# The last head group's probabilities go through DRAM like the others'; its scores are computed one weight granule earlier

## The reference, cut to what matters

```python
def moba_layer(x, norm_g, w_in, q_norm, k_norm, w_out):
    h = rms_norm(x, norm_g)
    q, k, v, z = jnp.split(h @ w_in, 4, axis=-1)      # w_in: 1024 x 8192
    q = rope(rms_norm(heads(q), q_norm))
    k = rope(rms_norm(heads(k), k_norm))
    v = heads(v)
    o = moba_attention(q, k, v)                        # softmax(q k^T * scale, causal) v
    return x + (o * jax.nn.silu(z)) @ w_out            # w_out: 2048 x 1024
```

## Time and profile before

| | |
|---|---|
| median of 3 runs | 412.7 us (412.46 to 412.87) |
| the profiled execution's own time | 412.65 us |
| its span | 410.7 us |
| TensorE busy in the span | 406.4 us (99%) |
| VectorE, ScalarE busy | 305.2 us (74%), 238.0 us (58%) |
| mean granted TensorE clock | 1.000 |

### The profile page before, as it was taken

How to read it: one execution, slowest core, us unless ns; L and a number is a source line. 1 busy time by engine, 2 the same in 40 slices (tenths; PEclk the granted TensorE clock), 3 DMA queues, 4 the chain that set the end, 5 groups by cost and what they waited for, 6 DMA issues and landing times.

```text
span 410.7 us, 5546 instructions
## 1 busy us (share of the span) xinstructions
PE 406.4 (99%) x2058; PEld 347.3 (85%) x2058; DVE 305.2 (74%) x405; ACT 238.0 (58%) x430; POOL 32.8 (8%) x45
## 2 busy tenths in 40 slices
PE   8999999999999999999999999999999999999996
PEld 8989889898888888888888888888888888888885
DVE  3879996978998855666836989569896699955622
ACT  5745553433735635677737696477965779646310
POOL 0167000000000000121000210010100200000000
PEclk9999999999999999999999999999999999999999
DMA  7996869756479975368896598995999879890002
GB/s 254 387 354 211 268 219 332 274 206 204 134 240 333 315 227 184 104 204 222 283 316 194 166 302 254 327 293 154 285 278 310 266 230 295 269 321 3 2 0 102
DMA packets 57466, 95.70 MB, mean 233 GB/s; under 512 B 9952, under 2 KB 19296, under 8 KB 57440
## 3 DMA queue, kind: packets, MB, share of 16 engines
q1 hardware_dynamic: 56720, 94.29, 71.9%
q10 hardware_dynamic: 720, 1.07, 0.8%
HBM read 84.07 MB, written 11.27 MB: 232 GB/s over the span
## 4 chain that ended last, share of the span: by engine, by line
PE 99%; DVE 0%; issue 0%
PE acc L739 26%; PE acc L741 26%; PE acc L740 26%; PE acc L762 3%; PE acc L784 3%; PE acc L783 3%; PE acc L781 3%; PE aux L874 2%; PE acc L803 1%; PE aux L739 1%; PE aux L741 1%; PE aux L740 1%; PE aux L892 1%; PE aux L893 1%; PE aux L891 1%; PE aux L873 1%
## 5 line engine op out<-in xcount | busy, mean ns | idle before, releaser
L951 DVE TENSOR_TENSOR w_lo<-raw,w_hi 128x2048 fp32r<-128x2048 f32 x65 | 147.9, 2280 | 25.7 <-ACT w_hi L472 25.7
L472 ACT ACTIVATE w_hi<-raw 128x2048 fp32r<-128x2048 f32 x64 | 121.9, 1912 | 46.1 <-PE acc L741 25.1
L739 PE MATMUL acc<-w_hi,hT_hi 128*128 128x512 f32 x320 | 127.9, 400 | 0.0
L741 PE MATMUL acc<-w_hi,hT_lo 128*128 128x512 f32 x320 | 124.8, 390 | 0.0
L740 PE MATMUL acc<-w_lo,hT_hi 128*128 128x512 f32 x320 | 124.6, 389 | 0.0
L741 PEld LDWEIGHTS acc<-w_hi,hT_lo 128*128 128x128 f32 x320 | 60.1, 188 | 13.0
L740 PEld LDWEIGHTS acc<-w_lo,hT_hi 128*128 128x128 f32 x320 | 60.2, 188 | 12.0
L739 PEld LDWEIGHTS acc<-w_hi,hT_hi 128*128 128x128 f32 x320 | 60.2, 188 | 11.8
L739 PE MATMUL acc<-w_hi,aT_hi 128*128 128x512 f32 x144 | 57.0, 396 | 0.0
L741 PE MATMUL acc<-w_hi,aT_lo 128*128 128x512 f32 x144 | 56.1, 390 | 0.0
L740 PE MATMUL acc<-w_lo,aT_hi 128*128 128x512 f32 x144 | 56.1, 389 | 0.0
(11 more groups left out here) (138 smaller groups left out, 477.0 us busy)
## 6 DMA issues: line engine op xcount, KB each, us to landing
raw<-in_w_in_dram SPq DMA_DIRECT2D x46, 1024.0 KB, 6.7
raw<-in_w_out_dram SPq DMA_DIRECT2D x16, 1024.0 KB, 5.3
raw<-in_w_pool_dram SPq DMA_DIRECT2D x4, 1024.0 KB, 7.8
wide<-between SPq DMA_DIRECT2D x32, 128.0 KB, 5.5
between<-wide SPq DMA_DIRECT2D x8, 512.0 KB, 3.4
p_between<-p_blocks SPq DMA_DIRECT2D x12, 192.0 KB, 4.3
p_blocks<-p_between SPq DMA_DIRECT2D x48, 48.0 KB, 2.6
raw<-in_w_in_dram SPq DMA_DIRECT2D x8, 256.0 KB, 7.9
```

Of the source, the lines that this page charges most:

```text
L472: act.activation(w_hi[:, slot, :], raw[:, slot, :], ACT.Copy).then_inc(hi_made, 1)
L739: pe.matmul(a, shi, whi, start=first and k == 0, stop=False)
L741: ins = pe.matmul(a, slo, whi, start=False, stop=last and k == GK - 1)
L951: dve.tensor_tensor(w_lo[:, slot, :], raw[:, slot, :], w_hi[:, slot, :].bitcast(F32), ALU.subtract).then_inc(w_split, 1)
```

## The change: what it does

The last group's probabilities take the path of the others: DVE turns them in 32x32 blocks, SP stores and fetches them, ACT copies them from `p_blocks`. The twelve PE transposes go. `scores(last, 0)` stands before out 0 instead of inside it; inside granule out j stands `attend(last, j + 1)`, with the values three steps behind the scores, so that values stay where they were and scores come one granule earlier. ACT and DVE have their last stage reordered. On SP, the fetch of the last group's k comes ahead of a weight load (it was behind), head 0's store and fetch stand around the fetch of y1, ahead of the load of out 7, and the other heads' come after all loads.

```diff
@@ SP, moves(g, j)
+                if (g, j) == (GROUPS, 0):
+                    store_p(g - 1, 0)
                 if j == 0 and g >= 2:
                     fetch_y1(g - 2)
+                if (g, j) == (GROUPS, 0):
+                    fetch_p(g - 1, 0)
...
-                if j == 6 and g < GROUPS:
+                if j == (6 if g < GROUPS - 1 else 5) and g < GROUPS:
                     fetch_k(g)
@@ SP, after the loads
+            last = GROUPS - 1
+            for h in range(1, HPG):
+                store_p(last, h)
+                fetch_p(last, h)
@@ ACT, exp_scores and probs_out
-                if g == GROUPS - 1 and h > 0:
-                    act.wait_ge(p_turned, h)
-                elif HPG * g + h > 0:
+                if HPG * g + h > 0:
                     act.wait_ge(p_blocked, HPG * g + h)
...
-                if g == GROUPS - 1:
-                    act.wait_ge(p_turned, h + 1)
-                else:
-                    act.wait_ge(p_landed, MOVED * (HPG * g + h + 1))
+                act.wait_ge(p_landed, MOVED * (HPG * g + h + 1))
                 if HPG * g + h > 0:
                     act.wait_ge(o_ready, HPG * g + h)
-                if g == GROUPS - 1:
-                    act.activation(probsT[:, :], aux[2][:, 0:3 * P], ACT.Copy).then_inc(pT_made, 1)
@@ ACT, last stage
-            for n in range(N_OUT1 + 3, N_END):
-                static_hi(n)
-                j = n - N_OUT1 - 3
-                if j < HPG:
-                    exp_scores(last, j)
-                if 1 <= j <= HPG:
-                    probs_out(last, j - 1)
+            exp_scores(last, 0)
+            for j in range(5):
+                static_hi(N_OUT1 + 3 + j)
+                if j + 1 < HPG:
+                    exp_scores(last, j + 1)
                 if j == 2:
                     y1_hi(last - 1)
+                if j >= 2:
+                    probs_out(last, j - 2)
+            probs_out(last, 3)
             y1_hi_last()
@@ PE
-            def turn_probs(g, h):
-                pe.wait_ge(exp_made, HPG * g + h + 1)
-                if h > 0:
-                    pe.wait_ge(pT_made, HPG * g + h)
-                for i in range(3):
-                    ins = pe.transpose(aux[2][:, i * P:(i + 1) * P], probs[:, i * P:(i + 1) * P], ident[:, :])
-                ins.then_inc(p_turned, 1)
...
             def attend(g, j):
-                late = 2 if g == GROUPS - 1 else 3
-                if j < HPG:
+                if 0 <= j < HPG:
                     scores(g, j)
-                if late <= j < HPG + late:
-                    values(g, j - late)
-                if g == GROUPS - 1 and 1 <= j < HPG + 1:
-                    turn_probs(g, j - 1)
+                if 3 <= j < HPG + 3:
+                    values(g, j - 3)
...
             last = GROUPS - 1
+            attend(last, 0)
...
-                inside = {6: lambda: turn_y1_last(1), 7: None}.get(j, lambda: attend(last, j))
+                inside = {6: lambda: turn_y1_last(1), 7: None}.get(j, lambda: attend(last, j + 1))
@@ DVE, last stage
             last = GROUPS - 1
+            head_max(last, 0)
             dve.wait_ge(gate_made, TT * 2 * GROUPS)
             for j in range(6):
                 if j < HPG:
-                    head_max(last, j)
-                if j == 5:
-                    y1_lo_bank(last, 0)
-                if j >= 2:
-                    head_out(last, j - 2)
+                    turn_probs(last, j)
                 n = N_OUT1 + 3 + j
                 if n < N_END:
                     weight_lo(n, n % RING)
+                if j + 1 < HPG:
+                    head_max(last, j + 1)
+                if j == 5:
+                    y1_lo_bank(last, 0)
                 if j == 2:
                     y1_lo(last - 1)
+                if j >= 2:
+                    head_out(last, j - 2)
             y1_lo_bank(last, 1)
```

More of the change, by code:

```diff
@@ L221, in bass_hybrid_trunk @@
         scores_ready, bias_made, exp_made = sem("scores_ready"), sem("bias_made"), sem("exp_made")
-        p_turned, pT_made, o_ready, y1_made = sem("p_turned"), sem("pT_made"), sem("o_ready"), sem("y1_made")
+        pT_made, o_ready, y1_made = sem("pT_made"), sem("o_ready"), sem("y1_made")
         out_made, out_stored = sem("out_made"), sem("out_stored")
@@ L582, in probs_out @@
             def probs_out(g, h):
-                if g == GROUPS - 1:
-                    act.wait_ge(p_turned, h + 1)
-                else:
-                    act.wait_ge(p_landed, MOVED * (HPG * g + h + 1))
+                act.wait_ge(p_landed, MOVED * (HPG * g + h + 1))
                 if HPG * g + h > 0:
                     act.wait_ge(o_ready, HPG * g + h)
-                if g == GROUPS - 1:
-                    act.activation(probsT[:, :], aux[2][:, 0:3 * P], ACT.Copy).then_inc(pT_made, 1)
[L591 to L594, removed]
+                act.activation(probsT[:, :].rearrange("p (n a i) -> p n a i", n=3, i=Q),
+                               p_blocks[:, h, :].rearrange("p (a n i) -> p n a i", n=3, i=Q),
+                               ACT.Copy).then_inc(pT_made, 1)
             def qkv_evacuate(g, which, first=False):
```

## The result

The changed kernel takes 421.61 us (median of 6 executions, 420.43 to 421.66) against 412.63 for the kernel before: ratio 1.0193, 95% interval 1.0166 to 1.0221. The medians lie 9.0 us apart (a quotient of 1.022, at the upper end of the interval; one execution of the kernel before took 415.43 us and two of the changed one about 420.5). The sum had said 421.6. The profiled execution took 421.57 us, of which the span is 419.6.

What follows compares the result with a forecast made beforehand. The prediction took TensorE to bound the kernel, its chain 99% TensorE without waits in the last stage. It summed 412.65 + 7.9 (wait) + 2.4 (clock) - 1.3 (transposes) = 421.6 us, range 419.0 to 423.5.

Steps and rivals of the forecast that it cites:

- PE's saving, 1.3 us: Last stage: dropping four heads' transposes, 0.33 us each, takes 1.3 us off PE; scores are moved, not removed.
- The wait, 7.9 us: Inside out 2, PE stands from 373.7 to 381.6 at head 0's values, for ACT's copy behind head 3's exp.
- The loop of 6.1 us: ACT and DVE hand on exp, w_hi, w_lo and head_max, 6.1 us a head; exps run from 360.5 to 378.8.
- The 0.2 us allowed for the hand-over: Between ACT's copy of head 0 and PE's values: 0.2 us for hand-over and weight load, part of the wait.
- The lower bound of 4.1 us: Wait at head 0's values if DVE is not late at all: 4.1 us, the chain from head 3's scores.
- The clock, 2.4 us of 0 to 2.8: PE's clock falls to 1.2 GHz in the wait; the restart then loses 2.4 us, bounds 0 and 2.8.
- Head 0's trip: Head 0's probabilities through DRAM: stored at 362.1, landed 366.4, fetches issued by 368.1, landed about 371; in time.
- The last load: Load of out 7 on SP: goes out about 368.3, 4 us later, needed after 380; hidden.
- k: Last group's k fetch lands at 354.7 to 357.8, scores wanted at 356.09: PE waits 0 to 1.7 us, taken as 0.
- Head 3's trip: Head 3's blocks, turned about 383, are back from DRAM by 392; values stand not before 398, so no wait.
- Rival (c): A second wait, from head 3's trip over 6 us longer or copy 1 1.6 us late: 423 to 425; 0.04 shared.
- Rival (d): Head 0's copy is in time at 373.7, so only the transposes' saving remains: 411.35 us, faster; chance 0.02.

Runs made afterwards that it cites:

- e9: e6 run once more, beside e8 on one chip: 411.37 us against 412.58 for the kernel before, ratio 0.9984 (0.9953 to 1.0016).
- e4: The kernel after, with each granule's w_hi made before the exp on ScalarE, head 0's copy still behind exp 3: 418.67 us, ratio 1.014.
- e2: The kernel after, with 32 unread identity products on TensorE between head 3's scores and head 0's values: 418.99 us.
- e3: The kernel after, with ScalarE's copy of a head's probabilities put before the next head's exp and the y1 part: 414.77 us, ratio 1.005.
- e7: e6, with the fetch of the last group's k back behind the weight load: 413.61 us, ratio 1.0015 (0.9997 to 1.0033).
- e5: The kernel after, with w_hi one ahead of the exp and head 0's copy before head 3's exp: 412.53 us, ratio 0.9995.
- e8: e6, with head 0's store and fetch and head 1's store ahead of the y1 fetch on SyncE: 412.55 us, ratio 0.9998.
- e6: e5, with head 1's store ahead of head 0's fetch and the load of out 7: 412.23 us against 412.69, ratio 0.9979.
- e1: The kernel before, with each head's three transposes of probs on TensorE made twice: median 415.18 us, ratio 1.0053 (1.0027 to 1.0079).

## Why the prediction was right, step by step

**PE's saving, 1.3 us.** Right: 4 x 0.33, shown by doubling (1.29 more from the scores of head 0 to the last matmul) and by e9's last stage (54.6 to 53.3).

**The wait, 7.9 us.** Measured from the end of the scores' cost (373.80 + 0.66 = 374.46) to 382.06: 7.6. The loop of 6.1 us came out at 6.10; the start was forecast for 360.5 and was 361.15, but the whole stage lay 0.7 us later, so against the scores it was on time. The 0.2 us allowed for the hand-over were too much by 0.1. The lower bound of 4.1 us for the order alone holds: in e4 the same measure gives 4.7 (373.02 + 0.66 to 378.35), with VectorE still 0.8 us late for head 3 (`head_max` at 374.79, where 373.02 + 0.99 was possible).

**The clock, 2.4 us of 0 to 2.8.** Right in kind; 1.9 by the rows of the profiled execution. Half clock lasted 3.9 us after the restart. The row behind the figure does not carry what it was used for: the program's first matmuls started 203 ns apart, but the profile shows them at a granted clock of 1.00:

```profile
1.00:7.00 6.00, 5.96 (x30) 5.96 (x30) 0.00 (x0) 2.37 (x4) 0.58 (x4) 1.00 0.78 228
```

So nothing shows that half clock made those 2.8 us, and that 2.4 came near 1.9 is partly luck. The rule of the Trainium skill (TensorE: Matmul & The Clock Gate, Part 1), half rate after idling and full rate after activity, agrees: 1.00, 0.50, 1.00 in the three windows of the kernel after. At the start of the program, before any activity, the profile shows 1.00, which the rule does not explain.

**An error that hid the other two.** Wait and clock together were 0.8 us less than forecast, and 0.7 us came from where nothing was forecast: out 0 began at 357.4 instead of 356.8 (0.66 of scores behind 356.09), through 0.1 us at the start and a wait of 0.3 us and its surroundings in an earlier group. That the median met the sum to 0.01 us is luck; that it lies within 1 us is not.

**Covers.** Head 0's trip was forecast to land at 371; its fetch was issued from 368.44 (forecast 366.4; the store went out at 362.94 and took 5.5 us, not 4.3). Its DMAs took 2.0 us each and so had landed by 371.8, still before 374.5. The last load went out at 370.21, not 368.3, and held nothing up; the forecast measured it by landings of small fetches, while loads of 1 MB took a median of 5.3 to 7.8 us on the page before, which leaves the cover standing.

k is the cover that nearly failed. Its fetch went out from 352.06, 1.2 us later than forecast, and its last DMA, issued at 353.4, landed at 356.6, 0.2 us ahead of the scores (356.77). In the profiled executions of e2 and e3, with the same order up to there, TensorE did wait for k, 1.3 and 0.2 us. The forecast's range of 0 to 1.7 us was right, and so was the reason for leaving it out: in e2 the head maxima of head 0 started at 361.35, straight behind the gate on VectorE and well behind the scores of 359.43, so the wait was covered there, as forecast. In the repaired versions nothing covers it; e7 shows what it then costs.

Head 3's trip and the copies 1 to 3 made no second wait. Rival (c) did not happen in the kernel after; with the first wait removed, its mechanism appeared as the 0.3 to 0.5 us of e5 and e8.

**Rival (d).** The trip through DRAM would have allowed it: e5 and e6 have the same trip and no loss. What forbade it was the written order, as stated.

**Left open.** The executions of the repaired versions spread over more than 2 us while most of the kernel before's lie within 0.3 (its slowest reach 416.9). In each profile of them and of e1, e3 and e4 there is a wait of 0.3 to 2.8 us for a `w_hi` in the program's first matmuls, before any changed instruction; in the kernel before's profile there is none. The chain leads from that `w_hi` back to the landing of the input x: the DMA holds it for 5.0 us in e1, 4.8 in e9 and 6.6 in e6. What such a wait costs is less than its length, since the 30 matmuls ahead of it took less time (5.10 us in e1, 6.14 in the kernel before): the first weight matmul starts at 7.29 in the kernel before, at 7.38 in e1, 7.17 in e9 and 9.03 in e6. So the late landing explains 1.7 us of e6's profile; why x lands later in some executions, and what makes e1's median 1.2 us slower than its profile, was not tried.

## What to carry to other kernels

When an engine's order is rearranged, go to every wait on the bounding engine and follow what it waits for back through the written order of the other engines; if an instruction in between needs something that the bounding engine has issued only just before the wait, the wait is that whole round, whatever lead the data has. "One granule earlier" for the producer gave nothing, because the consumer's copy was put behind a later head's exp. Then ask whether two engines hand each other the next step in turn (here exp, `w_hi`, `w_lo`, `head_max`): such a loop has a period of its own, and taking one item of it ahead opens it. And an idle stretch on TensorE can cost its clock on top: 1.9 us behind the 7.4 here.

## What the runs showed of the hardware

The granted clock of TensorE around its waits: it stayed at 1.00 through the wait of 1.65 us in e3; in the waits of 4.5 us in e4 and 7.4 us in the kernel after it fell to 0.50, the lower level of 1.2 GHz. Thirty-two products that nobody reads, in place of 7 us of idling, kept it at 1.00 and made the kernel about 2 us faster.

Four fetches of 128 KB for k landed 2.7 to 3.2 us after issue when they went out ahead of a weight load of 1 MB (e6), and 5.2 to 5.5 us after it when they went out behind one (e7). Three 128x128 fp32 transposes in a dense stream of matmuls took 0.33 us of TensorE's time.
